# Dividing the transposed attention output instead of the probabilities: a change to a float32 transformer kernel on one Trainium2 core

## The reference, cut to what matters

```python
logits = einsum(q, k) * scale + bias
logits = where(mask, logits, -inf)
p = softmax(logits)              # swa_mixer: e / (sum(e) + exp(sink - m))
out = einsum(p, v)               # 16 heads of 64, then @ w_out
```

## Time and profile before

| what | value |
|---|---|
| median of 3 runs | 1881.98 us (1881.93 to 1882.49) |
| the profiled execution's own time | 1881.88 us |
| its span | 1880.0 us |
| PE busy | 1734.8 us (92%) |
| DVE busy | 1161.9 us (62%) |
| ACT busy | 921.1 us (49%) |
| POOL busy | 206.0 us (11%) |

### The profile page before, as it was taken

How to read it: one execution, slowest core, us unless ns; L and a number is a source line. 1 busy time by engine, 2 the same in 40 slices (tenths; PEclk the granted TensorE clock), 3 DMA queues, 4 the chain that set the end, 5 groups by cost and what they waited for, 6 DMA issues and landing times.

```text
span 1880.0 us, 26392 instructions
## 1 busy us (share of the span) xinstructions
PE 1734.8 (92%) x9356; PEld 1467.5 (78%) x9356; DVE 1161.9 (62%) x1905; ACT 921.1 (49%) x1495; POOL 206.0 (11%) x284
## 2 busy tenths in 40 slices
PE   7999999999999895999997999993899999689999
PEld 6889988887788684788885788872598888569887
DVE  6667454565778757656567666555565656666555
ACT  4552454544544534644455544454754445265443
POOL 3005420100000013100005100002000001040000
PEclk9989999999999985999998999997999999689999
DMA  8440046455555540366652366633066665115662
GB/s 274 117 135 1 1 146 186 139 169 178 170 181 185 179 141 12 102 191 189 189 185 84 102 189 190 189 118 111 13 202 189 190 190 163 56 50 183 188 187 86
DMA packets 158176, 270.28 MB, mean 144 GB/s; under 512 B 15164, under 2 KB 41227, under 8 KB 158091
## 3 DMA queue, kind: packets, MB, share of 16 engines
q1 hardware_dynamic: 156571, 263.35, 45.6%
q0 software_dynamic: 1504, 5.79, 0.9%
q10 hardware_dynamic: 16, 0.00, 0.0%
HBM read 268.04 MB, written 1.07 MB: 143 GB/s over the span
## 4 chain that ended last, share of the span: by engine, by line
PE 82%; DVE 9%; ACT 3%; POOL 3%; issue 1%; DMA 0%; DVEq 0%; ACTq 0%; POOLq 0%
PE p_AC L2252 11%; PE p_AC L2254 11%; PE p_AC L2253 11%; PE p_UP L2252 6%; PE p_UP L2254 6%; PE p_UP L2253 6%; PE p_TP L2285 5%; PE p_UP L2285 5%; PE p_TP L2321 4%; PE p_UP L2286 2%; PE p_TP L2286 2%; DVE t_wl L1791 1%; PE p_AC L1046 1%; POOL t_sm L1750 1%; POOL t_A L1768 1%
## 5 line engine op out<-in xcount | busy, mean ns | idle before, releaser
L1791 DVE TENSOR_TENSOR t_wl<-t_raw,t_wh 128x1024 fp32r<-128x1024 f32 (+2 forms) x524 | 609.2, 1170 | 517.0 <-ACT t_wh L1261 514.4
L1261 ACT ACTIVATE t_wh<-t_raw 128x1024 fp32r<-128x1024 f32 (+2 forms) x524 | 528.9, 1016 | 611.8 <-PE p_AC L2254 273.6
L2252 PE MATMUL p_AC<-t_wh,t_uTh 128*128 128x512 f32 x612 | 243.4, 398 | 15.7 <-DVE t_wl L1791 8.8
L2254 PE MATMUL p_AC<-t_wh,t_uTl 128*128 128x512 f32 x612 | 241.6, 395 | 0.0
L2253 PE MATMUL p_AC<-t_wl,t_uTh 128*128 128x512 f32 x612 | 241.5, 395 | 0.0
L2252 PE MATMUL p_UP<-t_wh,t_hT 128*128 128x512 f32 (+3 forms) x576 | 226.7, 394 | 10.1 <-DVE t_wl L1791 5.5
L2254 PE MATMUL p_UP<-t_wh,t_hT 128*128 128x512 f32 (+3 forms) x576 | 223.9, 389 | 0.0
L2253 PE MATMUL p_UP<-t_wl,t_hT 128*128 128x512 f32 (+3 forms) x576 | 223.7, 388 | 0.0
L2252 PEld LDWEIGHTS p_AC<-t_wh,t_uTh 128*128 128x128 f32 x612 | 116.7, 191 | 42.3 <-DVE t_uTl L1941 8.0
L2285 PE MATMUL p_TP<-t_hT,t_wh 128*128 128x512 f32 x384 | 144.4, 399 | 0.0
L2285 PE MATMUL p_UP<-t_hT,t_wh 128*128 128x512 f32 x384 | 144.1, 398 | 0.0
(11 more groups left out here) (339 smaller groups left out, 2746.6 us busy)
## 6 DMA issues: line engine op xcount, KB each, us to landing
t_raw<-in_w_up SPq DMA_DIRECT2D x128, 512.0 KB, 4.0
t_raw<-in_w_down SPq DMA_DIRECT2D x128, 512.0 KB, 3.9
t_raw<-in_w_in SPq DMA_DIRECT2D x72, 512.0 KB, 3.7
t_raw<-in_w_up SPq DMA_DIRECT2D x88, 256.0 KB, 4.0
t_raw<-in_a_w_in SPq DMA_DIRECT2D x26, 512.0 KB, 3.7
t_raw<-in_w_down SPq DMA_DIRECT2D x44, 256.0 KB, 3.2
t_raw<-in_a_w_out SPq DMA_DIRECT2D x16, 512.0 KB, 3.5
t_raw<-in_b_w_in SPq DMA_DIRECT2D x12, 512.0 KB, 3.8
```

What stands on the lines that cost most here:

```text
L1261: A_(wh[:, c % SPL, 0:size(c)], raw[:, c % RAW, 0:size(c)], ACT.Copy).then_inc(high_done, 1)
L1791: V.tensor_tensor(wl[:, c % SPL, 0:n], raw[:, c % RAW, 0:n], wh[:, c % SPL, 0:n].bitcast(F32), ALU.subtract).then_inc(split_done, 1)
L2252: M(outs[t], a_hi, w_hi[:, k, :], start=first and k == 0, stop=False)
L2254: ins = M(outs[t], a_lo, w_hi[:, k, :], start=False, stop=last and k == ch.nk - 1)
```

## The change

The sums no longer divide the probabilities. DVE's `normalise_pair` is gone from the attention cores (it stays in the forgetting attention of the first block). In its place DVE computes the reciprocals of a pair's sums, each of the four numbers of a partition written 64 times, into a 128x256 tile `rec_t` in `hid`. PE transposes that tile as a fourth transpose of each head, beside the three of the probabilities, into the last 128 columns of the same bank. ACT copies 128x512 instead of 128x384 for each head. DVE multiplies the 128x256 output of the pair, from PSUM, by the transposed reciprocals in `pts_t` and writes it to `on_t` in `hid`; high and low halves are made from there. `pts_t` has six buffers of 512 columns in place of four of 384, and ACT and DVE run one iteration longer. The transposes of the probabilities wait for the exponentials (`exp_done`), the fourth transpose for `rec_done`, and P times V for `on_done`.

```diff
 # ACT, att_core
-                for i in range(PAIRS + 3):
+                for i in range(PAIRS + 4):
...
-                        if i >= 4:
-                            act.wait_ge(ov_done, pb + i - 3)
+                        if i >= 5:
+                            act.wait_ge(on_done, pb + i - 4)
                         for h in (2 * i - 4, 2 * i - 3):
                             act.wait_ge(tr_done, hb + h + 1)
-                            A_(pts_t[:, h % 4, :], tpb(h % 2, 3 * P), ACT.Copy).then_inc(ev_done, 1)
-                    if i >= 3:
-                        act.wait_ge(ov_done, pb + i - 2)
-                        A_(hTh[:, i - 3, :], acc((i - 3) % 2, S), ACT.Copy).then_inc(oh_done, 1)
+                            A_(pts_t[:, h % 6, :], tpb(h % 2), ACT.Copy).then_inc(ev_done, 1)
+                    if i >= 4:
+                        act.wait_ge(on_done, pb + i - 3)
+                        A_(hTh[:, i - 4, :], on_t[:, i % 2, :], ACT.Copy).then_inc(oh_done, 1)
 # DVE, att_core
-                    V.tensor_tensor(hTl[:, p, :], acc(p % 2, S), hTh[:, p, :].bitcast(F32),
+                    V.tensor_tensor(hTl[:, p, :], on_t[:, p % 2, :], hTh[:, p, :].bitcast(F32),
                                     ALU.subtract).then_inc(ol_done, 1)
+                def output_norm(p):
+                    dve.wait_ge(ov_done, pb + p + 1)
+                    if p >= 2:
+                        dve.wait_ge(ol_done, pb + p - 1)
+                    V.tensor_tensor(on_t[:, p % 2, :].rearrange("p (t s) -> p t s", t=NT),
+                                    acc(p % 2, S).rearrange("p (t s) -> p t s", t=NT),
+                                    pts_t[:, 2 * p % 6:2 * p % 6 + 2, 3 * P:], ALU.mult).then_inc(on_done, 1)
...
-                    if 4 <= i < PAIRS:
-                        output_low(i - 4)
+                    if 4 <= i < PAIRS + 4:
+                        output_norm(i - 4)
                     if 1 <= i <= PAIRS:
                         h = 2 * i - 2
                         dve.wait_ge(exp_done, hb + h + 2)
-                        normalise_pair(h).then_inc(norm_done, 1)
-                    if i >= PAIRS:
-                        output_low(i - 4)
+                        if h >= 4:
+                            dve.wait_ge(tr_done, hb + h - 2)
+                        V.reciprocal(rec_t[:, h // 2 % 2, :].rearrange("p (t u e) -> p t u e", t=NT, u=2),
+                                     esum_v[:, :, h:h + 2].unsqueeze(3).broadcast_to([P, NT, 2, 64]))                            .then_inc(rec_done, 1)
+                    if i >= 5:
+                        output_low(i - 5)
 # PE, att_core
-                            pe.wait_ge(norm_done, pb + h // 2 + 1)
+                            pe.wait_ge(exp_done, hb + h + 1)
                             if h >= 2:
                                 pe.wait_ge(ev_done, hb + h - 1)
-                            transposes([(tpb(h % 2, P, s * P), lg_t[:, h % 6, LB[s]]) for s in range(3)], tr_done)
+                            for s in range(3):
+                                pe.transpose(tpb(h % 2, P, s * P), lg_t[:, h % 6, LB[s]], ident[:, :])
+                            pe.wait_ge(rec_done, pb + h // 2 + 1)
+                            transposes([(tpb(h % 2, P, 3 * P), rec_t[:, i % 2, h % 2 * P:(h % 2 + 1) * P])],
+                                       tr_done)
...
                         if p >= 2:
-                            pe.wait_ge(ol_done, pb + p - 1)
+                            pe.wait_ge(on_done, pb + p - 1)
```

More of the change, by code:

```diff
@@ L124, in build @@
         sm = sb("sm", [P, SMALL])
-        mhalf = sb("mhalf", [P, 64])
+        mhalf = sb("mhalf", [P, 32])
         lg_t = sb("lg", [P, 6, LGW])
-        pts_t = sb("pts", [P, 4, 3 * P])
+        pts_t = sb("pts", [P, 6, COLS])
         def slot(n, width=SLOT, off=0):
@@ L440, in build @@
         MT = (slice(0, P), slice(P, 3 * P))
+        on_t = hid[:, 0:2 * S].rearrange("p (b s) -> p b s", b=2)
+        rec_t = hid[:, 2 * S:4 * S].rearrange("p (b s) -> p b s", b=2)
         def score_bank(h):
@@ L447, in build @@
         exp_done = sem("exp_done")
-        norm_done = sem("norm_done")
+        rec_done = sem("reciprocals_done")
+        on_done = sem("on_pair_done")
         tr_done = sem("tr_done")
@@ L1347, in fox_core @@
                                 act.wait_ge(pv_done, h - 3)
-                            A_(pts_t[:, h % 4, :], tpb(h % 2, 3 * P), ACT.Copy).then_inc(pe_done, 1)
+                            A_(pts_t[:, h % 4, 0:3 * P], tpb(h % 2, 3 * P), ACT.Copy).then_inc(pe_done, 1)
                     if i >= 3:
@@ L1873, in output_low @@
                     dve.wait_ge(oh_done, pb + p + 1)
-                    V.tensor_tensor(hTl[:, p, :], acc(p % 2, S), hTh[:, p, :].bitcast(F32),
+                    V.tensor_tensor(hTl[:, p, :], on_t[:, p % 2, :], hTh[:, p, :].bitcast(F32),
                                     ALU.subtract).then_inc(ol_done, 1)
-                for i in range(PAIRS + 4):
+                def output_norm(p):
[5 more added lines that the diff above has]
+                                    pts_t[:, 2 * p % 6:2 * p % 6 + 2, 3 * P:], ALU.mult).then_inc(on_done, 1)
+                for i in range(PAIRS + 5):
                     if i < PAIRS:
@@ L2395, in att_core @@
                         if p >= 2:
-                            pe.wait_ge(ol_done, pb + p - 1)
+                            pe.wait_ge(on_done, pb + p - 1)
                         dst = lambda h: AC[64 * (h % 2):64 * (h % 2) + 64, (p % 2) * COLS:(p % 2) * COLS + S]
                         for h in (2 * p, 2 * p + 1):
-                            M(dst(h), c["v"](h, 0), pts_t[:, h % 4, 0:S], start=True, stop=False)
+                            M(dst(h), c["v"](h, 0), pts_t[:, h % 6, 0:S], start=True, stop=False)
                         for h in (2 * p, 2 * p + 1):
-                            last = M(dst(h)[:, P:S], c["v"](h, 1), pts_t[:, h % 4, S:3 * P], start=False, stop=True)
+                            last = M(dst(h)[:, P:S], c["v"](h, 1), pts_t[:, h % 6, S:3 * P], start=False, stop=True)
                         last.then_inc(ov_done, 1)
```

## The result

| what | value |
|---|---|
| changed kernel | 1891.3 us median of 5 runs (1890.96 to 1892.25) |
| kernel before, timed beside it | 1882.49 us median of 5 runs (1881.93 to 1884.34) |
| ratio | 1.0047, 95% interval 1.0032 to 1.0061 |
| the profiled execution's own time | 1890.96 us (span 1889.2; before 1881.88 and 1880.0) |

The change makes the kernel 0.47% slower, 8.8 us between the medians, where 7 were forecast.

The account below looks back on a forecast made before the run. No engine clearly bound the kernel before; DVE had no notable gap and would be the limit after. Cores +2.15, +0.2, +2.35 and +2.1 made +6.8, rounded to +7, on 1881.88: 1889 us, range 1884 to 1897.

Parts of the forecast that it names:

- The reciprocal: On DVE, 256 numbers for each partition, priced from the slope of three small sizes: 1.75 us, 32 times.
- DVE's iteration: DVE's loop after the change, without gaps: 3.47 us in cores 0, 2 and 3, 3.73 in core 1.
- the middle parts: Each core from masks of pair 4 to those of pair 7: +1.1, -1.0, +1.0, +1.0 us.
- ACT and POOL: ACT would wait for DVE some 0.3 us an iteration; POOL's bias adds would keep their short length.
- rival 3: Reciprocal dearer, 2.2 us each (1901 us), or blocking POOL for its whole length (1894 us); chance 0.10.
- Core 1's gain: Core 1's middle part, whose 11.86 us held a stretched multiply, would fall to 10.85, -1.0.
- The last part: Each core from masks of pair 7 to the projection's first matmul: 7.6 us, +0.55, core 1 +0.65.
- The first part: Each core's start, up to masks of pair 4: +0.5 us in cores 0, 1 and 3, +0.8 in core 2.
- Rival 1: Reciprocal on DVE cheap at 0.42 us, ACT's 3.2 us iteration the limit; sum about 0, 1882 us; chance 0.08.
- Rival 2: With a cheap reciprocal, PE's transposes run ahead and PE leaves its lower clock two iterations earlier: 1877 us; chance 0.04.
- Rival 4: PE, idle a quarter of the longer iteration, stays at the lower clock longer in one or two cores: 1892 us; chance 0.06.

Follow-up runs that it names:

- e2: Changed kernel with a reciprocal of only the four sums, spread by a 128x256 DVE copy; 1881.91 us, ratio 0.9998 to the kernel before.
- e12: Kernel before, with each ACT copy of pair i-2 put ahead of the exponentials of a head of pair i; 1881.88 us, ratio 0.9994.
- e6: e2 with ACT copying 384 columns in place of 512 from the seventh head on, new reciprocals left out; 1882.47 us, ratio 1.0002.
- e1: The changed kernel run once more, unaltered, as reference point; 1890.75 us, ratio 1.0049 to the kernel before.
- e10: e9 with each ACT copy of pair i-2 put ahead of the exponentials of a head of pair i; 1873.5 us, ratio 0.9954.
- e9: e2 with small reciprocal and copy put ahead of the output multiply in DVE's loop; 1883.44 us, ratio 1.0004.
- e4: e2 with the high half of the output made by DVE in place of ACT; 1884.97 us, ratio 1.001.

## Why the prediction was right

**The reciprocal.** Forecast 1.75 us from three small sizes, measured 1.744, 32 times. e2 shows that this one instruction carries the loss. The Trainium skill (VectorE: DVE Perf Modes, First, the fixed hardware budget) gives the reciprocal a repeat count of 8. As an estimate, 8 cycles of its 0.96 GHz would have made 8.3 ns a number; the runs show 6.25, which at that clock is six cycles, and not the six and a half of the prediction's text.

**DVE's iteration.** Forecast 3.47 us without gaps in cores 0, 2 and 3 and 3.73 in core 1; measured 3.38 in core 0 and 3.75 in core 1, and the middle parts follow: +0.86, -1.08, +0.75 and +0.77 for +1.1, -1.0, +1.0 and +1.0. The masks take 1.10 us in the iteration shown, not 1.12, and the low half holds DVE for 0.28, not 0.34.

**ACT and POOL.** ACT waits 0.24 us for DVE in an iteration (forecast 0.3). POOL's wider addition, whole kernel after:
```profile
L1771 POOL TENSOR_TENSOR t_A<-t_A x32: 717/737/743, 736.4 to 1673.3; 128x256 f32<-128x256 f32 x32
L1771 POOL TENSOR_TENSOR t_A<-t_A,t_wmask x16: 722/727/734, 1018.1 to 1042.3; 128x256 f32<-128x256 f32 x16
```
None is stretched, and this one lies wholly inside the reciprocal of 757.34:
```profile
758.12 0.74 POOL L1771 TENSOR_TENSOR t_A<-t_A 128x256 f32<-128x256 f32 x1
```
So the reciprocal doesn't shut POOL out, and rival 3 falls in both its halves.

**Core 1's gain was luck in part.** Its stretched multiply is gone, and the middle part is 1.08 us shorter, as forecast. But the 11.86 us before held a second thing, which the prediction didn't read. PE waited 2.07 us for that multiply, and then ran at its lower clock; its scores took 1.65 us for 0.93, and DVE waited 0.99 us for them. The kernel before, PE's row and the busy times with the granted clock:
```profile
1038.77 1.65 PE L2383 MATMUL p_UP<-t_A 64*128 64x128 f32 x8
...
1037.60:1040.47 2.87, 2.87 (x17) 1.53 (x14) 1.84 (x6) 2.46 (x10) 2.87 (x6) 0.50 0.02 6
```
In e12, where one multiply is stretched to 2.22 us too but the granted clock is 1.00 throughout, the same part takes 11.09. So some 0.8 us of the 1.08 may belong to one fall of the clock in one profile; with one profile of the kernel before this can't be settled.

**The last part was mis-sized.** Forecast +0.55 (core 1 +0.65), measured +1.03, +1.13, +1.02 and +1.04: 4.2 us in all for 2.3. DVE's chain to the end of the last reciprocal was nearly as summed (5.64 us for 5.56). From there the step said five transposes 0.65, "a copy with its waits 0.58", P times V 0.80; measured are 2.43 us for 2.03:
```profile
765.41 1.09 ACT L1375 ACTIVATE t_pts<-p_TP 128x512 f32<-128x512 f32 x2 [0.86 <-PE p_TP L2335]
```
Both copies of the pair stand behind the last reciprocal, one after the other, 1.09 us, where the sum took one. e6, which made these copies narrower, shortened the last part by 0.3 to 0.43 us, which agrees.

**The first part.** Forecast +0.5, +0.5, +0.8 and +0.5, measured +0.35, +0.43, +0.80 and +0.40, and +0.89, +0.71, +0.80 and +0.46 in e1's profile of the same kernel.

**The errors offset each other in part.** The middle parts came to 0.8 us less than forecast, the last parts to 1.9 more, the first to 0.3 less. The mechanism was right, and the nearness of +7.5 to +6.8 is in part luck.

**Outside the cores** the sum had nothing, and 1.6 us came. Cores +7.5 for +6.8 and this give the 9.1. e1 shows that stretches ahead of the cores move by more than that with the same kernel, so this remainder is not put down to the change.

**Rival 1's condition** could be tried: with a cheap reciprocal it gave 1882 us, and e2 measured 1881.91. That it hit so closely is luck in part. It put the middle parts at 9.6 in cores 0, 1 and 3 by an ACT iteration of 3.2 us; they are 9.00, 9.35 and 9.00, and ACT's iteration in e2's core 0 is 3.02 (exponentials of pairs 6 and 7 from 750.89 and 753.91). The last parts rose by 0.6 to 0.8 and not by 0.5. Rival 2, a cheap reciprocal that makes the kernel faster, failed in e2 too; the gain needed another order on ACT.

**Rival 4**, PE at its lower clock for longer, did not come: the granted clock is 1.00 in every middle and last part of the changed kernel, in both of its profiles, and 0.57, 0.68, 1.00 and 0.59 in the first parts of its first profile for 0.57, 0.69, 1.00 and 0.59 before. In e1's profile it is 0.54 in the first parts of cores 0 and 1, which are 0.5 and 0.3 us longer than in the first.

## What to carry to other kernels

Broadcasting before a costly elementwise operation costs the operation at the full width: take the reciprocal of the few numbers and spread the result. Where taking work off the full engine gives nothing, as in e2, follow the work through every engine's order; the next limit may be an order and not an engine, and two edits that are each worth nothing can be worth 6 to 9 us together. At the end of a stage, count serial copies behind the last producer one by one.

## What the runs showed that was not expected

**A few dips of the clock move the same kernel by 5 us.** The changed kernel twice, same code, window 420 to 480 us (busy times of PE, PEld, DVE, ACT, POOL, then granted clock), first profile:
```profile
420.00:480.00 60.00, 54.54 (x237) 44.45 (x236) 35.19 (x50) 28.44 (x40) 2.65 (x4) 0.91 0.52 166
```
and e1:
```profile
420.00:480.00 60.00, 56.03 (x266) 46.52 (x267) 38.87 (x57) 28.88 (x40) 2.64 (x4) 1.00 0.58 185
```
The mean of 0.91 lies between the two levels of 1.2 and 2.4 GHz: part of the window ran at the lower one. Taken instruction by instruction, e1 is ahead by 2.0 us from 64 us on (the granted clock from 60 to 70 us is 0.92 in the first profile and 1.00 in e1), by 2.3 at 425 us and by 6.4 at 481 us, and then loses 1 us again by 666 us, so that core 0 starts 5.4 us earlier (731.83 for 737.26). The window above holds 4 of them. No attention core is near.

The kernel before has such a window too (0.94, core 0 at 737.03). In the 14 profiles core 0 starts at 731.8 to 731.9 four times, at 734.5 twice and at 737.0 to 737.5 eight times. e10 is among the four, e9 and the kernel before are not: of the 11.3 us between the spans of e10 and of the kernel before, 5.2 are there and 5.9 in the cores. So single profiles of the same kernel differ by more than half of what this change costs, and stretches must be compared from a start of their own, as the parts above are.

**A copy of 128x256 from SBUF to SBUF** takes 293 to 784 ns in e2. Those of core 2, where POOL is idle, take 0.29 us, and e4's cast takes 0.28 without POOL and 0.81 beside it; the reciprocal, of the same shape and with one input, stays within 1% at 1.74 us beside the same POOL.
